# One core, hybrid mixer and expert block: the experts and the per-layer embedding in one program, the projection of p moved ahead of the gates, tails in halves

## The reference, cut to what matters

```python
x = x + hierarchical_moe(rms_norm(x, ln_moe), ...)        # sum over k of gate[k] * y[k]
hp = rms_norm(x, ln_ple)
ple_gate = sigmoid(einsum('bsd,de->bse', hp, w_ple_gate))  # 1024 x 1024 x 1024
ple = einsum('bsp,pd->bsd', p, w_ple_proj)                 # 1024 x 256 x 1024
x = x + ple_gate * ple
return rms_norm(x, ln_final)
```

## Time and profile before

| | us |
|---|---|
| median of 3 runs | 1684.44 |
| lowest and highest | 1684.34, 1688.67 |
| the profiled execution, its time | 1688.82 |
| its span, first to last instruction | 1687.1 |
| PE busy in the span | 1446.6 (86%) |
| DVE, ACT, POOL busy | 510.7, 361.8, 261.9 |
| mean granted TensorE clock | 0.931 |
| the experts end with PE's last down matmul | 1490.1 |
| the block of the embedding begins | 1500.8 |

### The profile page before, as it was taken

How to read it: one execution, slowest core, us unless ns; L and a number is a source line. 1 busy time by engine, 2 the same in 40 slices (tenths; PEclk the granted TensorE clock), 3 DMA queues, 4 the chain that set the end, 5 groups by cost and what they waited for, 6 DMA issues and landing times. The chain is left out here.

```text
span 1687.1 us, 17290 instructions
## 1 busy us (share of the span) xinstructions
PE 1446.6 (86%) x6018; PEld 772.1 (46%) x6018; DVE 510.7 (30%) x695; ACT 361.8 (21%) x655; POOL 261.9 (16%) x379
## 2 busy tenths in 40 slices
PE   6999999789989999999994577778787878739997
PEld 4456844434467777774553322223232322214443
DVE  3332033325047666662223211111111111121332
ACT  2221131000044555551221000100010001022221
POOL 1000000100034344432110211111111111100110
PEclk9999999789999999999997698989998989879999
DMA  4221046522331211106110499999999999951220
GB/s 179 75 75 51 1 160 168 146 63 80 75 133 43 65 38 44 37 1 271 52 51 29 175 384 408 390 392 411 393 408 403 403 404 401 394 225 41 81 81 37
DMA packets 107334, 306.45 MB, mean 182 GB/s; under 512 B 22416, under 2 KB 60960, under 8 KB 81440
## 3 DMA queue, kind: packets, MB, share of 16 engines
q1 hardware_dynamic: 97792, 289.16, 45.6%
q0 software_dynamic: 9504, 16.80, 2.6%
HBM read 283.85 MB, written 39.90 MB: 192 GB/s over the span
## 5 line engine op out<-in xcount | busy, mean ns | idle before, releaser
L1532 PE MATMUL pe_gu<-w_gu,xT 128*64 128x512 f32 x1024 | 273.5, 695 | 109.1 <-DMA w_gu<-in_w_expert_up 105.7
L251 PE MATMUL ps<-wide,gst 128*128 128x512 f32 x640 | 284.7, 605 | 2.7 <-DVE wide L404 2.7
L1532 PEld LDWEIGHTS pe_gu<-w_gu,xT 128*64 128x64 f32 x1024 | 83.2, 159 | 277.7 <-issue 275.9
L251 PEld LDWEIGHTS ps<-wide,gst 128*128 128x128 f32 x640 | 123.4, 195 | 153.9 <-issue 152.1
L832 DVE TENSOR_TENSOR_SCAN Pm<-rem,Pm 128x128 f32<-128x128 f32 (+3 forms) x96 | 108.0, 1125 | 76.4 <-ACT brk L766 76.3
L1625 DVE TENSOR_TENSOR hs<-sg,pe_gu 128x256 f32<-128x256 f32 x32 | 13.5, 421 | 382.3 <-ACT sg L1596 382.3
L1193 PE MATMUL p_x<-wide,mT 128*128 128x512 f32 x256 | 114.8, 602 | 2.1 <-DVE mx L1125 1.4
L1550 PE MATMUL pe_y<-w_d,hTe 128*64 128x512 f32 x512 | 115.4, 592 | 1.1 <-DVE ys L1630 1.1
L1853 PE MATMUL f_pg<-w_gu,f_xT 128*128 128x512 f32 x256 | 115.2, 604 | 1.1 <-ACT f_xT L1771 1.1
L928 POOL TENSOR_TENSOR wt<-brk,Pm 128x128 f32<-128x128 f32 (+3 forms) x96 | 88.7, 923 | 164.5 <-DVE Pm L832 164.5
L265 PE MATMUL psk<-w_tok,wide 128*128 128x260 f32 (+1 forms) x384 | 111.7, 453 | 0.0
(11 more groups left out here) (281 smaller groups left out, 1490.5 us busy)
## 6 DMA issues: line engine op xcount, KB each, us to landing
w_gu<-in_w_expert_gate SPq DMA_DIRECT2D x64, 1024.0 KB, 14.0
w_gu<-in_w_expert_up SPq DMA_DIRECT2D x64, 1024.0 KB, 16.1
w_d<-in_w_expert_down SPq DMA_DIRECT2D x64, 1024.0 KB, 9.3
gst<-in_w_in SPq DMA_DIRECT2D x20, 512.0 KB, 4.3
y_sb<-y_d SPq DMA_DIRECT2D x8, 1024.0 KB, 5.3
qkv_d<-y_sb SPq DMA_DIRECT2D x12, 512.0 KB, 2.6
qk_st<-rows_d SPq DMA_DIRECT2D x8, 768.0 KB, 7.1
gst<-qkv_d SPq DMA_DIRECT2D x8, 768.0 KB, 5.4
```

The source lines that it names most:

```text
L251: last = pe.matmul(ps[s][:, c], w_ct[:, s, k, :], hT[:, k, c], start=k == 0, stop=k == KT - 1)
L1532: last = pe.matmul(p_gu[e * CAP:(e + 1) * CAP, :], xT[:, s, k, e * CAP:(e + 1) * CAP], wv[:, e, :, k, :], start=k == 0, stop=k == KT - 1)
```

## The change

The two stages become one block, `stage_experts_and_embedding`, without the barrier between them, and its buffers are laid over those of the experts. All loops over the tiles are written out. In detail:

- SP: lnp is loaded before w_ple_gate. When the last gate-up group is done, it loads all of p (`p_all`, 1 MB), w_p and lnf into the second half of `w_gu`, all on one semaphore. Then it waits for the last scatters itself and loads y of tiles 0 and 1.
- PE: transposes p tile by tile and projects all eight tiles of p before the first gate; the halves go round four banks of PSUM. The transposes of x of tile 0 stand before the last projection. A tile then is gate(t, 0), the transposes of x of t+1, gate(t, 1).
- DVE: copies each half of the projection into `e_sb` in SBUF (`take_e`), with mix and norm of tiles 0 and 1 in between. The multiply and the add after the gate run by halves of 512 columns, and per tile the order is add_e(t), mix(t+2), norm(t+2), finish(t).
- ACT: the eight scalings are mixed with the copies of transposed p; the sigmoid runs by halves.
- POOL: the same small roots, in the same order.

```diff
@@ SP @@
-                sp.dma_start(w_g, A["w_ple_gate"][0]...).then_inc(ple_in, 16)
                 sp.dma_start(lnp[:], A["ln_ple"][0]...).then_inc(ple_in, 16)
+                sp.dma_start(w_g, A["w_ple_gate"][0]...).then_inc(ple_in, 16)
+                sp.wait_ge(gu_done, n * NP + 1)
+                sp.dma_start(p_all, A["p"][0, 0]...).then_inc(p_in, 16)
+                sp.dma_start(w_p, A["w_ple_proj"][0]...).then_inc(p_in, 16)
+                sp.dma_start(lnf, A["ln_final"]...to_broadcast([P, D])).then_inc(p_in, 16)
+                for s in range(2):
+                    sp.wait_ge(y_out[s], n * (NPS * 16) + 16)
+                load_y(0)
+                load_y(1)
+                for t in range(NT):
+                    if t + 2 < NT:
+                        sp.wait_ge(x2_ok, t + 1)
+                        load_y(t + 2)
+                    sp.wait_ge(o_ok, t + 1)
+                    sp.dma_start(out_v[:, t, :], o_sb[:, t % 2]).then_inc(out_done[t % 2], 16)
@@ PE @@
+                def embed(t):
+                    pe.wait_ge(pT_ok, t + 1)
+                    for h in range(2):
+                        i = 2 * t + h
+                        if i >= 4:
+                            pe.wait_ge(e_ok, i - 3)
+                        for k in range(PT):
+                            last = pe.matmul(p_e[i % 4], pT[:, t % 2, k, :], half(w_p[:, k, :], h), ...)
+                        last.then_inc(e_done, 1)
+                turn_p(0)
+                turn_p(1)
+                pe.wait_ge(ys_ok, n * NP + 1)
+                for t in range(NT - 1):
+                    embed(t)
+                    if t + 2 < NT:
+                        turn_p(t + 2)
+                turn_x(0)
+                embed(NT - 1)
+                pe.wait_ge(wg_ok, KT)
+                for t in range(NT):
+                    gate(t, 0)
+                    if t + 1 < NT:
+                        turn_x(t + 1)
+                    gate(t, 1)
@@ ACT @@
+                copy_p(0)
+                copy_p(1)
                 act.wait_ge(ple_in, 32)
                 for k in range(KT):
-                    act.activation(w_g[:, k, :], w_g[:, k, :], ACT.Copy, scale=lnp[:, k:k + 1])
+                    act.activation(w_g[:, k, :], ...).then_inc(wg_ok, 1)
+                    if k % 2:
+                        copy_p(k // 2 + 2)
+                for t in range(KT // 2 + 2, NT - 1):
+                    copy_p(t)
+                first_squares(0)
+                copy_p(NT - 1)
+                copy_x(0)
+                for t in range(NT):
+                    if t + 1 < NT:
+                        first_squares(t + 1)
+                    sigmoid(t, 0)
+                    if t + 1 < NT:
+                        copy_x(t + 1)
+                    sigmoid(t, 1)
+                    act.wait_ge(x3_ok, 2 * t + 2)
+                    ...
+                    squares(t, 1, s3_ok)
@@ DVE @@
+                def add_e(t):
+                    for h in range(2):
+                        dve.wait_ge(gt_ok, 2 * t + h + 1)
+                        dve.wait_ge(e_ok, 2 * t + h + 1)
+                        dve.tensor_tensor(half(gt, h), half(gt, h), half(e_sb[:, t, :], h), ALU.mult)
+                        dve.wait_ge(ge_ok, 2 * t + h + 1)
+                        dve.tensor_tensor(half(x_sb[:, t, :], h), half(x_sb[:, t, :], h), half(gt, h), ALU.add)
+                for t in range(NT // 2):
+                    take_e(t)
+                mix(0)
+                take_e(4)
+                norm(0)
+                take_e(5)
+                mix(1)
+                take_e(6)
+                norm(1)
+                take_e(7)
+                for t in range(NT):
+                    add_e(t)
+                    if t + 2 < NT:
+                        mix(t + 2)
+                        norm(t + 2)
+                    finish(t)
```

More of the change, by code:

```diff
@@ L1509, in one_pass, with rms @@
                     pairs(pool, lambda: None, body, last)
-                n = passes(pool, one_pass)
-                for s in range(2):
-                    pool.wait_ge(y_out[s], n * (NPS * 16) + 16)
+                passes(pool, one_pass)
+                pool.memset(nh[:], -0.5).then_inc(nh_ok, 1)
+                pool.wait_ge(nh_ok, 1)
+                def rms(t, n, summed, mid, done):
+                    c = ss[:, t % 2, n:n + 1]
+                    pool.wait_ge(summed, t + 1)
+                    pool.tensor_scalar(c, c, 1.0 / D, EPS, ALU.mult, ALU.add).then_inc(mid, 1)
+                    pool.wait_ge(mid, t + 1)
+                    pool.tensor_tensor(c, c, nh[:], ALU.pow).then_inc(done, 1)
+                rms(0, 0, s2_ok, r2_step, r2_ok)
+                for t in range(NT):
+                    if t + 1 < NT:
+                        rms(t + 1, 0, s2_ok, r2_step, r2_ok)
+                    rms(t, 1, s3_ok, r3_step, r3_ok)
             @block.tensor
@@ L1585, in _, with turn_p, turn_x, gate @@
                 pe.wait_ge(pset, 8)
-                passes(pe, one_pass)
+                n = passes(pe, one_pass)
+                def turn_p(t):
+                    if t == 0:
+                        pe.wait_ge(p_in, 48)
+                    if t >= 2:
+                        pe.wait_ge(pT_ok, t - 1)
+                    for k in range(PT):
+                        last = pe.transpose(p_t[t % 2][:, k, :], p_all[:, t, k::PT], ident[:])
+                    last.then_inc(pt_done, 1)
+                def embed(t):
[4 more added lines that the diff above has]
+                            pe.wait_ge(e_ok, i - 3)
+                        for k in range(PT):
+                            last = pe.matmul(p_e[i % 4], pT[:, t % 2, k, :], half(w_p[:, k, :], h), start=k == 0, stop=k == PT - 1)
+                        last.then_inc(e_done, 1)
+                def turn_x(t):
+                    pe.wait_ge(xn_ok, t + 1)
+                    if t >= 1:
+                        pe.wait_ge(fT_ok, t)
+                    for k in range(KT):
+                        last = pe.transpose(p_x[:, k, :], xn[:, t % 2, k::KT], ident[:])
+                    last.then_inc(ft_done, 1)
+                def gate(t, h):
+                    pe.wait_ge(fT_ok, t + 1)
+                    if t == 0:
+                        pe.wait_ge(e_ok, 2 * NT - 3 + h)
+                    else:
+                        pe.wait_ge(gt_ok, 2 * t - 1 + h)
+                    for k in range(KT):
+                        last = pe.matmul(half(p_y, h), fT[:, t % 2, k, :], half(w_g[:, k, :], h), start=k == 0, stop=k == KT - 1)
+                    last.then_inc(g_done, 1)
+                turn_p(0)
[13 more added lines that the diff above has]
+                    gate(t, 1)
             @block.scalar
@@ new lines, in copy_x, with sigmoid, first_squares @@
+                def copy_x(t):
+                    act.wait_ge(ft_done, t + 1)
+                    act.activation(flat(fT[:, t % 2]), flat(p_x[:]), ACT.Copy).then_inc(fT_ok, 1)
+                def sigmoid(t, h):
+                    act.wait_ge(g_done, 2 * t + h + 1)
+                    if t >= 1:
+                        act.wait_ge(x3_ok, 2 * t - 1 + h)
+                    act.activation(half(gt, h), half(p_y, h), ACT.Sigmoid).then_inc(gt_ok, 1)
+                def first_squares(t):
+                    act.wait_ge(x2_ok, t + 1)
+                    if t >= 1:
+                        act.wait_ge(s2_ok, t)
+                    if t >= 2:
+                        act.wait_ge(s3_ok, t - 1)
+                        act.wait_ge(xn_ok, t - 1)
+                    squares(t, 0, s2_ok)
@@ L1671, in _ @@
                 passes(dve, one_pass)
[L1674 to L1780, removed]
-                    act.activation(sq[:], xrow(t), ACT.Square, accum_out=ss[:, s, 1:2]).then_inc(s3_ok, 1)
-                def step(t, s, half_t, first, last):
-                    if not last:
-                        before_next(t, s)
-                    after(t, s, first)
-                def before_next(t, s):
-                    if not (isinstance(t, int) and t == 0):
-                        act.wait_ge(s3_ok, t)
-                    before(t + 1, 1 - s, False)
-                before(0, 0, True)
-                tiles_skewed(act, step)
-            @block.vector
-            def _(dve):
-                def combine(t, s, nth):
-                    dve.wait_ge(y_in[s], nth * 16 + 16)
-                    dve.scalar_tensor_tensor(xrow(t), y_sb[:, s, 0], gates[:, 0, ds(t, 1)], xrow(t), ALU.mult, ALU.add).then_inc(x2_step, 1)
@@ L1802, in combine, with norm @@
+                def norm(t):
                     dve.wait_ge(r2_ok, t + 1)
[L1803 to L1812 removed]
```

147 lines of the change are left out of this document (71 added, 76 removed).

## The result

| | us, median (lowest to highest) | ratio to the kernel before, 95% interval |
|---|---|---|
| before, measured beside it | 1684.91 (1684.34 to 1688.67) | 1 |
| changed | 1661.89 (1656.52 to 1662.80) | 0.9852 (0.9827 to 0.9878) |

A forecast was written before the change was run, and what follows sets the result against it. Experts were bound by weight loads, the last stage by PE and its waits. Lead-in +7.7, first tile -6.4, six periods -24.0, last tile with tail -4.0 sum to -26.7; summed directly 26.9 less, median 1657.5, range 1649 to 1669.

The forecast's parts named there:

- I take the difference that the change makes off the median: Whole kernel: the 26.9 us summed in the profiled execution are subtracted from the median 1684.4, giving 1657.5.
- The lead-in: Experts to first gate matmul: loads in at 1493.5, projections from 1494.9, first gate matmul at 1526.8, 7.7 us later.
- the 2.0 us for the clock: Start of the projections: PE's pause of 1490.1 to 1493.6 costs 2.0 us of slow clock, bounds nothing and 3.0.
- The rival of a longer chain or lead-in: Tiles and lead-in: half operations priced as whole ones, or p_in at 1497 and another clock step; 1662 to 1668, chance 0.18.
- The rival of a clock that stays low: Projection and tiles: PE's pauses keep or bring back the lower clock; 1700 at full loss, chance 0.04.
- The tile: Last stage's tiles: projection gone, the chain to xn sets the period, 16.0 us instead of 20.0.
- the `passed` increments are gone ... nothing: ACT and POOL in the tiles: removing these semaphore increments changes nothing, being beside other work.
- The wait that stays: Each later tile, before the transposes: PE still waits 1.25 us for xn, as the chain takes 8.1 us.
- The tail: From the last gate matmul to the end: 9.0 us, where before it was 3.44 of projection and 9.5.
- before 1512: Lead-in, a sign to see in the profile: ACT's scalings of the gate weights end before 1512.
- Idle not filled: Rival, lead-in: PE reaches the projections only when y and the norm are ready; median 1677, chance 0.04.
- first tile: First gate tile: tile 1 already normed in the lead-in, so 14.7 us for 21.1, -6.4.

The follow-up runs named there:

- e7: Changed kernel with the increments of `passed` put back before the squares on ACT and the root on POOL; 1658.80 us in one execution.
- e1: Changed kernel with the sigmoid, multiply and add after the gate on whole tiles of 1024 columns again; 1674.06 us, ratio 0.992.
- e4: Changed kernel with mix(t+2) between the two halves of add_e(t) on DVE and loads of y one tile earlier; 1654.10 us, ratio 0.9815.
- e9: Changed kernel with ln_final on its own semaphore, p loaded ahead of w_ple_gate, and mix between the halves of add_e; 1645.32 us, ratio 0.9758.
- e10: The changed kernel run once more with nothing edited; 1660.24 us, ratio 0.9838.
- e5: Changed kernel with only tile 0 projected ahead and the projection of t+1 behind the second half of gate(t); 1666.75 us, ratio 0.9884.
- e3: Changed kernel with p, w_p and ln_final loaded ahead of w_ple_gate, into the weight buffer half that frees first; 1651.99 us, ratio 0.9797.
- e6: Changed kernel with p, w_p and ln_final loaded only once the last scatters have landed, ahead of y; 1668.89 us, ratio 0.989.

## Why the prediction was right, and where its terms were off

The direction, the range and the rhythm were right. The forecast was 1657.5 and the median is 1661.9.

- *The median.* "I take the difference that the change makes off the median" is the step that was off, by the whole 4 us. The two profiled executions differ by 26.9, as summed, but the medians by 23.0: the profiled execution before (1688.82) stood 4.4 above its median, and the one after (1661.92) stands at its own. In the one before the experts ended 3.5 us later (D 1486.4 for 1483.0). In the old kernel all that follows stands behind the barrier and so behind D, while in the changed one PE's return hangs on the loads, whose first, w_ple_gate, was issued at the same time in both (1469.89 and 1469.66). That would account for 3.5 of the 4.4, but it rests on one profile of the kernel before and is not shown.
- *The lead-in.* The projections were to start at 1494.9 and start at 1495.92. All three loads stand in one row behind w_ple_gate, as argued, and are in at 1494.6 instead of 1493.5. But the experts ended 3.5 us earlier than in the sum, so that PE's pause is 8.05 us, not the 3.5 on which the 2.0 us for the clock rested; it cost 2.8. G: 1528.35 for 1526.8.
- *The rival of a longer chain or lead-in.* The median of 1661.9 lies at its lower end (1662 to 1668), and by the time alone it could have come true. By the timeline the chain was shorter than forecast and only the lead-in longer, by 1.5 us, with the loads in at 1494.6 and not at 1497.
- *The clock.* The rival of a clock that stays low is refuted: 1.00 from 1502 to 1650, through the rotation over four banks. What the Trainium skill's "TensorE: Matmul & The Clock Gate", section "A second HAM failure mode: psum-queue depth-cycling", reports did not happen here. The section has short idle times between the groups, and in this projection PE has none from 1502 to 1528 (26.00 us busy of 26.00), so the run shows only that going round four banks by itself costs no clock.
- *The tile.* Forecast 16.0, measured 15.57. The half operations came out as interpolated (0.60, 0.69, 0.69). The stretch from mix to transposes, which "the change doesn't touch", took 5.55 us and not 5.93: the step "the `passed` increments are gone ... nothing" failed. They stand on that very chain, and e7 gives them 0.2 of the 0.38. Over six tiles the term was 2.6 us too high.
- *The wait that stays.* That the chain and not PE ends the tile was right: 0.68 us of wait for the 1.25 forecast. e1 lengthens the chain and the period follows; e4 shortens it and PE's own 14.6 us remain.
- *The tail.* Forecast 9.0, measured 10.1 (from 1650.1 to 1660.2). The part up to the end of the last output tile was 5.6 us, 0.3 shorter than forecast. The rest is at the very end, in the waits of SP, first before, then changed:

```profile
SPq L1711 <- PEq L1711: 0.2, 1, 0.2
```

```profile
SPq L1456 <- PEq L1456: 1.5, 1, 1.5
```

  SP is done with the last store and waits 1.5 us for PE to close the block, in e1 to e7, e9 and e10 as well as in the changed kernel. PE's last matmul was 10 us earlier. Why it arrives late wasn't tried and stays open.
- *Nothing hidden came out.* The copies to SBUF, the scalings of w_ple_gate (last at 1512.2, forecast 1510) and y were all off the path, as costed; only the sign "before 1512" for the scalings was missed, by 0.2 us. "Idle not filled" is refuted by the timeline; its price is not e5's, where the projections were moved back into the tiles.

The terms +1.5 (lead-in), -0.1 (first tile), -2.6 (six periods) and +1.1 (tail) cancel to -0.1. That the span came out exact was luck; the mechanism, PE filled ahead of the gates and a tile that ends with the chain to xn, is what the timelines show.

## What to carry to other kernels

When two stages are merged to fill an engine's idle time, ask which load ends that idle time and what stands ahead of it in the queue: here exchanging the order of p and w_ple_gate brought another 7 to 9 us (e3), about a third of what the whole merge had. Work that leaves a tile also uncovers what it hid, so compare the tile's chain with the engine's own work before and after; halves (e1) and the place of an independent step in an in-order stream (e4) then decide. Take the difference of two spans for what it is: where a DMA-bound stage lies ahead, mark its end in both profiles before crediting the rest to the edit.

## What the runs showed that I had not expected

- The end of the experts, which no edit touches, lay between 1478.1 and 1486.4 us in the twelve profiled executions. PE's gate-up groups of the last pairs took either 7.1 us (full clock) or 8.4 to 9.9, with waits for weights of 1.5 to 5.5 us ahead of them. The last group alone moves D: it starts at 1470.88 in the changed kernel and at 1470.80 in e6, takes 7.09 and 8.78 us, and D is 1482.96 and 1484.57.
- Of the two small instructions of a root on POOL, one takes longer where it runs beside the second step of DVE's mix. In the kernel before it is the first (1.12 us for 0.19), in the changed kernel the second (1.39 for 0.55):

```profile
1546.46 1.30 DVE L1847 SCALAR_TENSOR_TENSOR mx<-wide_tab,gates,mx 128x1024 f32<-128x1024 f32 x1
...
1546.77 1.39 POOL L1567 TENSOR_TENSOR f_ss<-f_ss,f_nh 128x1 f32<-128x1 f32 x1
```

  The first one starts at 1546.50 there, 0.04 us into the mix step, and takes 0.19 us as ever. The groups (busy, mean ns) of the changed kernel give 867 and 190 ns, where the kernel before had 552 and 553. With e4's order neither runs beside the mix, and they take 550 and 190; no run changes the mix alone, so that it is the cause is likely and not shown. The changed kernel:

```profile
L1567 POOL TENSOR_TENSOR f_ss<-f_ss,f_nh 128x1 f32<-128x1 f32 x16 | 13.9, 867 | 1.3
...
L1565 POOL TENSOR_SCALAR f_ss<-f_ss 128x1 f32<-128x1 f32 x16 | 3.0, 190 | 145.3 <-ACT w_gu L1725 145.3
```

  It costs nothing here: the stretched ones belong to the root for the output tile, while the one on the chain runs when DVE waits for it.
